# The back part of an encoder block on one core: MLP blocks in pairs by halves of the tokens, norms batched by four tiles, the last gate product bank by bank

## The reference, cut to what matters

```
mix = concat(a, r) @ w_o                                # 1024 x 1024
x = x + rmsnorm(mix, norm_mix_post)
h = rmsnorm(x, norm_mlp_pre)
m = square(relu(h @ w_up)) @ w_down                     # width 4096 between
x = x + rmsnorm(m, norm_mlp_post)
e = p @ w_ple                                           # 256 x 1024
gate = sigmoid(x @ w_ple_gate)                          # 1024 x 1024
x = x + rmsnorm(e * gate, norm_ple)
```

## Time and profile before

| | |
|---|---|
| median of 3 timed runs | 1569.44 us (1569.37 to 1571.33) |
| the profiled execution | 1566.52 us |
| its span, first to last instruction | 1564.7 us |
| PE busy, share of the span | 1490.6 us, 95% |
| mean granted TensorE clock | 0.986 of full speed |

### The profile page before, as it was taken

How to read it: one execution, slowest core, us unless ns; L and a number is a source line. 1 busy time by engine, 2 the same in 40 slices (tenths; PEclk the granted TensorE clock), 3 DMA queues, 4 the chain that set the end, 5 groups by cost and what they waited for, 6 DMA issues and landing times.

```text
span 1564.7 us, 18619 instructions
## 1 busy us (share of the span) xinstructions
PE 1490.6 (95%) x7192; PEld 1214.2 (78%) x7192; DVE 659.9 (42%) x977; ACT 476.6 (30%) x908; POOL 519.2 (33%) x448
## 2 busy tenths in 40 slices
PE   6999998999999999998899999999999999998996
PEld 5878888778657778777788888888888888876774
DVE  6135545645576764436313223051513223057253
ACT  5223323123255554444212121121212121143442
POOL 3273544355000014544222222222222222254462
PEclk9999998999999999999999999999999999999998
DMA  5221010102230006222211111111111111132233
GB/s 188 63 67 41 21 41 14 24 22 68 61 81 1 1 1 209 82 80 91 65 47 48 53 48 48 48 47 48 48 54 47 47 48 47 48 109 67 82 89 133
DMA packets 65670, 94.91 MB, mean 61 GB/s; under 512 B 12720, under 2 KB 29104, under 8 KB 65584
## 3 DMA queue, kind: packets, MB, share of 16 engines
q1 hardware_dynamic: 65584, 93.74, 20.1%
HBM read 87.43 MB, written 4.19 MB: 59 GB/s over the span
## 4 chain that ended last, share of the span: by engine, by line
PE 85%; DVE 6%; issue 4%; POOL 3%; ACT 1%; DMA 0%; SPq 0%; DVEq 0%; ACTq 0%
PE ps L50 23%; PE ps L51 22%; PE ps L52 22%; PE ps L909 3%; PE ps L1368 3%; PE ps L1386 3%; PE ps L1376 2%; DVE hid_low L1657 1%; PE ps L1228 1%; PE ps L1000 1%; POOL wy_low L1175 1%; POOL y_stat L1577 1%; PE ps L939 1%; PE ps L954 1%; POOL wx_low L365 0%
## 5 line engine op out<-in xcount | busy, mean ns | idle before, releaser
L1175 POOL TENSOR_TENSOR wy_low<-w_raw,wy_high 128x512 fp32r<-128x512 f32 x216 | 296.5, 1374 | 623.2 <-ACT wy_high L1162 623.2
L1162 ACT ACTIVATE wy_high<-w_raw 128x512 fp32r<-128x512 f32 x216 | 136.3, 631 | 657.6 <-PE ps L52 653.1
L50 PE MATMUL ps<-wy_high,hid_high 128*128 128x512 f32 x512 | 202.2, 395 | 14.3 <-DVE hid_low L1657 6.1
L50 PE MATMUL ps<-a_high,wy_high 128*128 128x512 f32 x512 | 200.2, 391 | 1.7 <-DVE a_low L1182 1.7
L51 PE MATMUL ps<-wy_low,hid_high 128*128 128x512 f32 x512 | 200.7, 392 | 0.0
L52 PE MATMUL ps<-wy_high,hid_low 128*128 128x512 f32 x512 | 200.5, 392 | 0.0
L51 PE MATMUL ps<-a_low,wy_high 128*128 128x512 f32 x512 | 199.9, 390 | 0.0
L52 PE MATMUL ps<-a_high,wy_low 128*128 128x512 f32 x512 | 199.8, 390 | 0.0
L1641 DVE TENSOR_SCALAR relu<-ps 128x512 f32<-128x512 f32 x32 | 21.9, 686 | 284.0 <-PE ps L52 283.5
L1682 DVE TENSOR_TENSOR total<-total,ps 128x512 f32<-128x512 f32 x112 | 75.8, 687 | 152.5 <-PE ps L52 152.5
L365 POOL TENSOR_TENSOR wx_low<-w_raw,wx_high 128x512 fp32r<-128x512 f32 (+1 forms) x64 | 82.3, 1290 | 140.8 <-ACT wx_high L466 140.8
(11 more groups left out here) (188 smaller groups left out, 2432.7 us busy)
## 6 DMA issues: line engine op xcount, KB each, us to landing
w_raw<-in_w_up SPq DMA_DIRECT2D x72, 256.0 KB, 2.7
w_raw<-in_w_down SPq DMA_DIRECT2D x72, 256.0 KB, 2.6
w_raw<-in_w_in SPq DMA_DIRECT2D x62, 256.0 KB, 2.8
w_raw<-in_w_o SPq DMA_DIRECT2D x32, 256.0 KB, 2.6
w_raw<-in_w_ple_gate SPq DMA_DIRECT2D x32, 256.0 KB, 2.6
x_tile<-in_x SPq DMA_DIRECT2D x8, 512.0 KB, 8.2
x_res<-in_x SPq DMA_DIRECT2D x8, 512.0 KB, 5.1
y<-x_res SPq DMA_DIRECT2D x8, 512.0 KB, 3.2
```

The source lines that it names most:

```text
L50: pe.matmul(out, stat_high, mov_high, start=start, stop=False)
L1162: act.activation(wy_high[:, n % PAIRS, :], w_raw[:, n % RING, :], ACT.Copy).then_inc(high_made, 1)
L1175: pool.tensor_tensor(wy_low[:, n % PAIRS, :], w_raw[:, n % RING, :], wy_high[:, n % PAIRS, :].bitcast(F32), ALU.subtract).then_inc(low_mad ...
```

## The change

The MLP goes in four pairs of blocks, each pair for token half 0 and then for token half 1: two up4 segments (block f, block f + 1), then two down segments "dp" of 8 tiles, one for each column half, that add both blocks in PSUM. Each of these segments has 12 matmuls per weight tile, so that every weight tile of the MLP is loaded and split twice, once per token half. The hidden parts are now laid out as two slots (block even or odd) of one token half each.

The norms' small steps (sums, means, roots) take four tiles in one instruction, and the places of the transposes, ACT's and DVE's orders and the banks are new. The junk outputs of ACT's squares go to buffers of their own.

In the gate part, the segments are gate, gate, e, e for half 0, then gate, e, e for half 1, and last "gr", the second column half's gate product of token half 1. Its eight weight tiles ("res") are split ahead, into the places of `a_high` and `a_low` that token half 0 has left, after the tiles named in `res_after`. "gr" then runs bank by bank, that is all of k for one token tile before the next. The product with the norm's gain is made beside ACT's square, and the final addition and the store of y go by column halves (256 KB each).

The diff, cut to its core:

```diff
-            segs += [("up4", 0, 0, 0), ("up4", 0, 1, 0), ("dn8", 0, 0, 0), ("dn8", 0, 0, 1)]
-            for f in range(1, 7):
...
+            for f in (0, 2, 4, 6):
+                for h in range(2):
+                    segs += [("up4", f, h, 0), ("up4", f + 1, h, 0), ("dp", f, h, 0), ("dp", f, h, 1)]
+            segs += [("gate", 0, 0, 0), ("gate", 0, 0, 1), ("e", 0, 0, 0), ("e", 0, 0, 1)]
+            segs += [("gate", 0, 1, 0), ("e", 0, 1, 0), ("e", 0, 1, 1), ("gr", 0, 1, 1)]
+            depth = {"wo": 8, "up4": 8, "up8": 8, "dn8": 4, "dp": 8, "gate": 8, "e": 2, "gr": 0}
...
-                    return [4 * h + i for i in range(4)]
+                    return [4 * (f % 2) + i for i in range(4)]
                 if kind == "up8":
                     return [4 * (q % 2) + q // 2 for q in range(8)]
                 if kind == "dn8":
                     return list(range(8))
-                if kind == "dn4":
-                    return [4 * (h == 0 and n == 1) + i for i in range(4)]
...
+                if kind == "dp":
+                    return [4 * n + i for i in range(4)]
+                if kind == "gate":
+                    return [4 * n + i for i in range(4)]
+                return [4 * ((n + h) % 2 if kind == "e" else 1) + i for i in range(4)]
...
             before = {(0, 1): [(0, 4)], (0, 2): [(0, 5)], (0, 3): [(0, 6)], (0, 4): [(0, 7)],
-                      (2, 4): [(1, 0)], (2, 6): [(1, 1)], (3, 1): [(1, 2)], (3, 3): [(1, 3)],
-                      (4, 4): [(1, 4)], (4, 5): [(1, 5)], (4, 7): [(1, 6)], (5, 0): [(1, 7)],
...
+                      (2, 6): [(1, 0)], (3, 2): [(1, 1)], (3, 4): [(1, 2)], (3, 6): [(1, 3)],
+                      (U00, 6): [(1, 4)], (U10, 2): [(1, 5)], (U10, 4): [(1, 6)], (U10, 6): [(1, 7)],
+                      (U71, 3): [(2, 0)], (U71, 5): [(2, 1)], (D10, 3): [(2, 2)], (D10, 5): [(2, 3)],
+                      (G00, 2): [(3, n) for n in range(4)], (G00, 6): [(2, 4)],
+                      (G01, 1): [(2, 5)], (G01, 3): [(2, 6)], (G01, 5): [(2, 7)]}
+            turned_at = {b: [turn for turn in turns if turn[0] in (1, 2)] for b, turns in before.items()}
+            turn_bank = [[6, 6, 6, 6, 4, 6, 4, 6], [4, 0, 2, 0, 4, 0, 2, 0], [0, 2, 4, 6, 4, 0, 2, 0], [4, 5, 6, 7]]
...
+            res_after = {first[E01]: [0], first[E01] + 1: [1]}
+            res_after.update({first[G10] + k: [k + 1] for k in range(1, 7)})
+            stream, place = [], {}
+            for n in range(TILES):
+                for tile in [("pair", n)] + [("res", r) for r in res_after.get(n, [])]:
+                    place[tile] = len(stream)
+                    stream.append(tile)
...
+            def high_of(act, tile):
+                q = place[tile]
+                act.wait_ge(loaded[q % RING], 16 * (q // RING + 1))
+                if tile[0] == "res":
+                    act.wait_ge(done, done_at["bank", G01, 7, 3])
+                    out = a_high[:, 0, tile[1], :]
+                else:
+                    out = wy_high[:, tile[1] % PAIRS, :]
+                    if tile[1] >= PAIRS:
+                        act.wait_ge(done, done_at["tile", tile[1] - PAIRS])
+                act.activation(out, w_raw[:, q % RING, :], ACT.Copy).then_inc(high_made, 1)
+
             def high(act, n):
-                if n >= TILES:
-                    return
...
+                if n < TILES:
+                    high_of(act, ("pair", n))
+                    for r in res_after.get(n, []):
+                        high_of(act, ("res", r))
...
                 for t in range(TT):
-                    sp.wait_ge(added9, t + 1)
-                    sp.dma_start(y[t * P:(t + 1) * P, :], x_res[:, t, :]).then_inc(stored, 16)
...
+                    for n in range(2):
+                        cols = slice(n * BANK, (n + 1) * BANK)
+                        sp.wait_ge(added9, 2 * t + n + 1)
+                        sp.dma_start(y[t * P:(t + 1) * P, cols], x_res[:, t, cols]).then_inc(stored, 16)
+                sp.wait_ge(stored, 16 * 2 * TT)
...
+                            squares7x(2 * (s - 2) + k - 2)
+                        if behind == "up4" and k < 2:
+                            if s == U10 and k == 0:
+                                act.wait_ge(evicted, 16)
+                            if s == D00 and k == 0:
+                                act.wait_ge(tile7_made, TT)
+                            hidden_half(s - 1, k)
+                        if s == U61 and k < 4:
+                            squares8(k)
+                        if s == G00 and k < 2:
+                            squares8(4 + 2 * k)
+                            squares8(5 + 2 * k)
+                        if s == G00 and k == 3:
+                            for i in range(4):
+                                act.wait_ge(done, done_at["turn", 3, i, 0])
+                                act.activation(p_high[:, i // 2, i % 2 * BANK:(i % 2 + 1) * BANK],
+                                               ps[:, turn_bank[3][i], :], ACT.Copy).then_inc(p_high_made, 1)
+                        if s == G01 and k == 0:
+                            gates(0, 0)
+                        if s == E00 and k == 0:
+                            gates(0, 1)
+                        if s == G10 and k in (1, 2):
                             squares9(0, k - 1)
-                        if n == 1 and k == 0:
+                        if s == E10 and k == 0:
                             gates(1, 0)
-                s = seg_at["e", 0, 1, 0]
-                high(act, first[s] + AHEAD)
...
+                        for stage, t in turned_at.get((s, k), []):
+                            turned(act, stage, t)
                 squares9(1, 0)
-                squares9(1, 1)
+                for i in range(4):
+                    gate_of(1, 1, i)
+                    square9_of(1, 1, i)
...
+                    for h in range(2):
+                        four = slice(4 * h, 4 * h + 4)
+                        if (s, k) == ((2, U00)[h], 1):
+                            roots_of(sum7_made, h + 1, sum7, rstd7, rstd7_made, four)
+                        if (s, k) == ((2, U00)[h], 4):
+                            roots_of(mean7x_made, h + 1, mean7x, rstd7x, rstd7x_made, four)
+                        if (s, k) == ((U61, 3), (G00, 2))[h]:
+                            roots_of(mean8_made, h + 1, mean8, rstd8, rstd8_made, four)
+                    if (s, k) == (G10, 3):
+                        roots_of(sum9_made, 1, sum9, rstd9, rstd9_made, slice(0, 4))
...
+                def product_of(h, n, i):
                     s = seg_at["e", 0, h, n]
-                    for i in range(4):
-                        dve.wait_ge(done, done_at["bank", s, 1, i])
...
+                    c9 = 8 * h + 4 * n + i
+                    here = total[:, 4 * h + i, n * BANK:(n + 1) * BANK]
+                    dve.wait_ge(done, done_at["bank", s, 1, i])
+                    dve.wait_ge(gate_made, c9 + 1)
+                    dve.wait_ge(added8, 4 * h + i + 1)
+                    dve.tensor_tensor(here, ps[:, banks_of(s)[i], :], gate[:, n, i, :], ALU.mult).then_inc(product, 1)
+                    dve.wait_ge(product, c9 + 1)
+                    dve.tensor_tensor(gate[:, n, i, :], here, gain_ple[:, n * BANK:(n + 1) * BANK],
+                                      ALU.mult).then_inc(scaled9, 1)
+
+                def sum9_of(tiles, squares):
...
+                    dve.wait_ge(rstd9_made, max(1, t - 2))
+                    dve.wait_ge(scaled9, 8 * (t // 4) + 4 + t % 4 + 1)
+                    for n in range(2):
+                        here = x_res[:, t, n * BANK:(n + 1) * BANK]
+                        dve.scalar_tensor_tensor(out=here, in0=gate[:, n, t % 4, :], scalar=rstd9[:, t:t + 1], in1=here,
...
+                    sums7(h)
                     for t in range(4):
-                        sum7_of(o + t)
-                    add7(o)
...
+                        add7(o + t)
+                    means7x(h)
                     if h == 0:
                         dve.wait_ge(pre_in, 16)
                     tile7(o)
-                    add7(o + 2)
-                    mean7x_of(o + 1)
                     tile7(o + 1)
                     low_of(dve, 1, o)
-                    add7(o + 3)
-                    mean7x_of(o + 2)
...
+                for s in range(U10, U61):
+                    if segs[s][0] in ("up4", "up8"):
+                        hidden_all(s)
                     else:
-                        for q in range(1, 8, 2):
-                            hidden(seg_at["up8", f, 0, 0], q, 8 * f + q)
...
+                        add_down(s)
                 dve.wait_ge(mlp_in, 16)
+                means8(0)
                 for t in range(4):
-                    mean8_of(t)
-                add8(0)
...
+                    add8(t)
+                hidden_all(U61)
                 low_of(dve, 2, 0)
-                add8(3)
                 low_of(dve, 2, 1)
```

(76 more changed lines are left out.)

440 lines of the change are left out of this document (187 added, 253 removed).

## The result

The changed kernel took 1527.27 us (median of 4, 1526.39 to 1527.86) against 1569.4 us (median of 4): ratio 0.9729, interval 0.9712 to 0.9746, that is 42 us less.

What follows compares the result with a forecast made beforehand. TensorE, busy 1490.6 of 1564.7 us, bounds, so only its waits, slow clock and tail can be won. Its end, 1549.4 - 42.4 gaps plus remaining costs, is 1517.5; plus 7.7 tail, span 1525, 39.5 less: median 1530, range 1523 to 1544.

Steps and rivals of the forecast that it cites:

- TensorE's work: Whole back part: TensorE's work does not change, 3744 matmuls from 642.25 on, 848.6 us.
- the weights split twice: MLP: each tile feeds 12 matmuls, 2.72 us, not 24; cost nothing, covered by a slack of 3.3 us.
- Rival 3: MLP seams: narrow weight stream becomes the bound, ACT's third high part 6 us late at 15 seams; 1571; chance 0.04.
- no change: MLP seams: some 2.5 us lost at each, like the narrow-stream rival but milder; chance 0.03.
- Seams and banks: MLP seams: waits for relu (2.1), hid_low (6.1), a_low (1.7) go; different banks remove the 5.9 us wait at 1413.
- The norm after w_o: Transposes two tiles later, batched by four: h_tile waits 2.3 us twice, 4.6 in place of 7.4.
- one slow stretch: Before 757 us: 1.5 us allowed for one stretch of slow clock in place of three (5.8); bounds 0 and 4.
- Rival 2: Norm batches later than forecast: two places each wait 5 us and cost 2 of slow clock; 1538; chance 0.14.
- The gate products: Sigmoid waits of 1.9 go, 0.4 comes; ahead-split makes G10's weights late by 2.3 us, bounds 0 and 8.
- Rival 1: G10: POOL bounds it, every subtraction meets a DVE instruction and takes 2.18; 8 us, so 1536; chance 0.16.
- The end: Last gate product bank by bank, then a half-sized store: tail 7.7 us for 15.2; bounds 6.5 and 11.
- The sum: Whole kernel: TensorE's end 1517.5 plus 7.7 gives span 1525, 39.5 less; median 1530.

Runs made afterwards that it cites:

- the first run on the kernel before: Kernel before, with DVE adding up the third of the last four down segments ahead of the first two norm additions: 1569.21 us, ratio 0.9999.
- The two runs there: Changed kernel with the second norm's mean and root tile by tile: 1518.79 us; with the batch kept and first transposes one weight tile later: 1518.50 us.
- the next doubling: Changed kernel with POOL doing the subtraction of each of the MLP's 256 weight tiles twice: 1561.43 us.
- the run with two edits: Kernel before, third down segment added up before the norm additions, and two low parts of the gate's input before the last down segment's bank additions: 1562.61 us.

## Why the prediction was right, point by point

**TensorE's work, the weights split twice.** As forecast: same count, 87.05 us per half block, no wait in the MLP, and 328 subtractions of POOL in place of 216. Wide blocks put back cost 2.55 us for 2.5 expected; that it is so near is luck, since the runs of one kernel spread over 1.7. Rival 3 and no change are out.

**Seams and banks.** All of the earlier trace rows but h_tile and the low part is gone, and 0.6 for a sigmoid is new. For the wait of 5.9 us the order on DVE was the cause, as I had it; no run has other banks with the old order. That the wait alone is worth 5.9 does not hold, as the first run on the kernel before shows. Here the forecast is right because the whole seam was rearranged. That the waits for hid_low (6.1) and a_low (1.7) went with the pairs by token halves is argued from the order; the trace shows them gone, and no run takes them apart.

**The norm after w_o.** The step's chain was right and two terms were too small. The wait is 2.7, not 2.3, twice: the root of four tiles took 1.01 us where I put 0.54, the price of one tile's. The groups by form of POOL, 642 to 1526 us, show it (count, busy and mean ns):

```profile
L1608 POOL TENSOR_TENSOR y_stat<-y_stat,minus_half 128x4 f32<-128x4 f32 x7 | 7.1, 1007 | 2.5 <-DVE y_stat L1653 2.2
L1608 POOL TENSOR_TENSOR y_stat<-y_stat,minus_half 128x1 f32<-128x1 f32 x4 | 2.2, 546 | 27.6 <-DVE y_stat L1742 27.6
```

Counted from the step's start, the accumulator and the mean came where I had them, h_tile later by what the root took more, with the subtraction in its way as forecast (2.2 us). And I allowed one slow stretch, 1.5 us; there were two, 3.4 us. Rival 2 was thus true in part: 5.4 + 3.4 against my 4.6 + 1.5. The two runs there show that the waits and the slow clock together cost 8 us.

**The gate products.** Waits for the low part 0.6 us, 1.2 with restarts, for my 2.3. A subtraction that met one of DVE's 0.69 us instructions took 1.74 (mostly), not the 2.0 I put at most. Rival 1 needed 2.18 for each. The wait of 0.4 at 1483 us is of the kind I forecast, beside DVE's final additions. The one at 1480 us has a cause that I left out: POOL had stood 1.3 us for a high part that ACT made behind the eight squares of the norm, and then made the root of four, 1.0 us, first. The sigmoid's wait was 0.6 for my 0.4.

**The end.** 7.0 us for my 7.7: the store took 2.5 for 3.1. The order by banks is worth 9.5 us, more than the tail became shorter, since with the new instructions the old order has a tail of 16.0.

**The sum.** The forecast's terms add up to a span of 1525.2, and it was 1525.9. TensorE's part was 876.2 us, from 642.74 to 1518.9, for the forecast's 875.3: norm +2.7, gate -0.9, and another -0.9 in the small terms that I can't place. The end gave -0.7, and the front part, which the change doesn't touch, ended 0.5 us later in this execution. So the span is nearer than its terms, because the errors had both signs: that is luck. The median, 1527.3 for 1530, differs by more, since the difference of two profiled executions was set on a median from which one of them was 2.9 us away.

## What to carry to other kernels

Count what TensorE waits for at one seam as a whole: the duties behind a wait can be late by nearly as much, and one repair then moves the wait (0 us for one, 6.6 for two). When small steps are batched, the first consumer waits for the last producer; move the consumer by as much, one weight tile here, or leave the step on the critical path unbatched. An engine with room can take double work for nothing (POOL's busy share in the MLP went from 24% to 50% without a wait of TensorE), but the next doubling, to 97%, cost 35 us, since beside DVE its work takes longer than it does alone. A last product should end bank by bank when the chain behind a bank is shorter than the bank's matmuls.

## What the runs showed of the hardware that was not expected

POOL's power of -0.5 took 0.55 us on 128x1 and 1.01 on 128x4, so four in one are cheaper than four single ones, but what waits for the first gets it nearly twice as late. A POOL subtraction of 128x512 took 1.29 us alone and 1.74 when it met one DVE instruction of 0.69 us with two SBUF inputs, 0.45 more and so less than the whole of it; the DVE instruction took 1.07 there. Beside 1024-element ones the subtraction took 2.18. The same wait of 1.86 us before G01's first matmul was followed by a slow stretch in one of three kernels (1458 us in the run with one edit on the kernel before) and by none in the kernel before and in the run with two edits; the waits of 2.7 at about 662 and 713 us were followed by one each time, in seven traces. The wait of 3.7 for the first h_tile was followed by none in the kernel before (clock 1.00 from 657 to 662 us), and by one in the run with one edit (0.72 from 655 to 661).
